# A two-layer encoder trunk on one core: another order of the work up to the first attention

## The reference

```
h    = rms_norm(x, attn_norm)                        # 256 x 1024
c_q  = rms_norm(h @ w_dq, g_cq)                      # 1024 -> 384
q    = (c_q @ w_uq).reshape(B, S, 16, 96)            # 384 -> 1536
kv_a = h @ w_dkv                                     # 1024 -> 288
c_kv = rms_norm(kv_a[..., :256], g_ckv)
k_pe = broadcast(kv_a[:, :, None, 256:])             # 32 rotary columns
kv   = (c_kv @ w_ukv).reshape(B, S, 16, 64 + 64)     # 256 -> 2048
k_nope, v = kv[..., :64], kv[..., 64:]
q = rms_norm(q, g_qn); k = rms_norm(concat(k_nope, k_pe), g_kn)
q, k = rope on the last 32 columns of each
o = block_causal_attention(q, k, v, 96 ** -0.5)
x = x + o @ w_o
```

## Time and profile before

| | |
|---|---|
| median of 3 runs | 1473.21 us (1472.29 to 1474.28) |
| the profiled execution | 1474.44 us, span 1472.6 us |
| busy in the span | TensorE 1420.9 us (96%), VectorE 1123.0, ScalarE 950.7, GpSimd 208.3 |
| HBM read | 430.95 MB |
| granted TensorE clock, mean of the span | 0.987 |
| share of the chain that ended last | TensorE 88%, VectorE 5%, DMA 2%, ScalarE 2% |

### The profile page before, as it was taken

How to read it: one execution, slowest core, us unless ns; L and a number is a source line. 1 busy time by engine, 2 the same in 40 slices (tenths; PEclk the granted TensorE clock), 3 DMA queues, 4 the chain that set the end, 5 groups by cost and what they waited for, 6 DMA issues and landing times.

```text
span 1472.6 us, 19787 instructions
## 1 busy us (share of the span) xinstructions
PE 1420.9 (96%) x7123; PEld 1202.1 (82%) x7123; DVE 1123.0 (76%) x986; ACT 950.7 (65%) x911; POOL 208.3 (14%) x145
## 2 busy tenths in 40 slices
PE   5899999999999799999999999999999999999997
PEld 5688899997877688888888888888888888888885
DVE  4576544446675688898899899888888889889985
ACT  4455443335553577777787687778777778678762
POOL 3120100000010323004003001200500400300322
PEclk9999999999999999999999999999999999999998
DMA  8144565554552499999999999999999999999994
GB/s 290 67 140 147 182 198 175 196 177 146 191 177 81 136 349 385 376 383 383 395 359 385 403 351 383 405 341 396 399 359 400 383 378 378 383 394 356 388 403 182
DMA packets 155442, 441.73 MB, mean 300 GB/s; under 512 B 11806, under 2 KB 41675, under 8 KB 155403
## 3 DMA queue, kind: packets, MB, share of 16 engines
q1 hardware_dynamic: 147296, 422.49, 77.0%
q0 software_dynamic: 4656, 15.03, 2.8%
q10 hardware_dynamic: 3450, 3.69, 0.8%
HBM read 430.95 MB, written 13.38 MB: 302 GB/s over the span
## 4 chain that ended last, share of the span: by engine, by line
PE 88%; DVE 5%; DMA 2%; ACT 2%; issue 2%; POOL 1%; POOLq 0%; ACTq 0%; SPq 0%; DVEq 0%
PE ps L1494 81%; PE ps L1489 4%; PE ps L1614 2%; DVE wl_a L1015 1%; PE ps L1634 1%; DMA y_rows<-ye,cur_s 1%; DVE wl_b L1015 1%; ACT wh_a L684 0%; ACT tn L693 0%; PE ps L1835 0%; DMA xr<-in_x 0%; DVE tn L1021 0%; DMA bias<-bias_wide 0%; DVE htl L1034 0%; DMA tn<-tn_rows,cur_g 0%
## 5 line engine op out<-in xcount | busy, mean ns | idle before, releaser
L1015 DVE TENSOR_TENSOR wl_a<-raw,wh_a 128x2048 fp32r<-128x2048 f32 (+1 forms) x230 | 515.9, 2269 | 122.8 <-ACT wh_a L684 122.7
L684 ACT ACTIVATE wh_a<-raw 128x2048 fp32r<-128x2048 f32 (+1 forms) x230 | 433.2, 1908 | 199.5 <-PE ps L1494 171.5
L1015 DVE TENSOR_TENSOR wl_b<-raw,wh_b 128x2048 fp32r<-128x2048 f32 x168 | 376.8, 2286 | 39.9 <-ACT wh_b L684 39.8
L684 ACT ACTIVATE wh_b<-raw 128x2048 fp32r<-128x2048 f32 x168 | 318.5, 1927 | 37.4 <-PE ps L1494 22.9
L1494 PE MATMUL ps<-wh_a,hth 128*128 128x512 f32 (+2 forms) x576 | 225.4, 391 | 8.5 <-DVE htl L1034 4.1
L1494 PE MATMUL ps<-wh_a,htl 128*128 128x512 f32 (+2 forms) x576 | 223.6, 388 | 0.0
L1494 PE MATMUL ps<-wl_a,hth 128*128 128x512 f32 (+2 forms) x576 | 223.5, 388 | 0.0
L1494 PE MATMUL ps<-wh_b,hth 128*128 128x512 f32 x448 | 175.0, 391 | 0.0
L1494 PE MATMUL ps<-wh_b,htl 128*128 128x512 f32 x448 | 174.5, 389 | 0.0
L1494 PE MATMUL ps<-wl_b,hth 128*128 128x512 f32 x448 | 174.3, 389 | 0.0
L1494 PEld LDWEIGHTS ps<-wh_a,hth 128*128 128x128 f32 x576 | 109.4, 190 | 30.2 <-issue 6.5
(11 more groups left out here) (259 smaller groups left out, 2190.7 us busy)
## 6 DMA issues: line engine op xcount, KB each, us to landing
raw<-in_moe_w SPq DMA_DIRECT2D x336, 1024.0 KB, 8.4
raw<-in_ffn_w SPq DMA_DIRECT2D x33, 1024.0 KB, 5.3
raw<-in_a_w_o SPq DMA_DIRECT2D x4, 1024.0 KB, 5.9
raw<-in_b_w_q SPq DMA_DIRECT2D x4, 1024.0 KB, 5.0
raw<-in_kv_w_k SPq DMA_DIRECT2D x4, 1024.0 KB, 5.0
raw<-in_kv_w_v SPq DMA_DIRECT2D x4, 1024.0 KB, 5.0
raw<-in_b_w_o SPq DMA_DIRECT2D x4, 1024.0 KB, 5.1
bias<-bias_wide ACTq DMA_DIRECT2D x8, 384.0 KB, 3.2
```

Source lines behind the costliest of these rows:

```text
L684: nc.scalar.activation(dst[:, 0:w], raw[:, n % RAW, 0:w], ACT.Copy).then_inc(hi_done, 1)
L1015: nc.vector.tensor_tensor(l[:, 0:w], raw[:, n % RAW, 0:w], h[:, 0:w].bitcast(fp32), ALU.subtract).then_inc(lo_done, 1)
```

## The change

The mathematics stays; lines numbered from here on are those of the changed kernel. Its parts:

- TensorE starts with six filler products as soon as the constants are there; the gains' transpose goes ahead of the rows' transposes, its copy ahead of the second block's scaling. ScalarE squares each block of x as soon as that block has landed.
- `turn_out("n0")` goes in two halves, with the halves of unit 1 between them.
- The transposes of the first three latent chunks go between the two w_dkv units, those of the last two between the first and the second w_uq unit; their splits are placed to match. GpSimd's root for the query latents goes ahead of its rotary tables.
- w_ukv is multiplied in another order: the key columns of both units first (each product reads 8 runs of 64 columns, one after every 128), then the value columns. A new semaphore `k_proj` counts the key tiles. The squares and sums follow each tile.
- The last four copies (values) go to the end: ScalarE's two ahead of `head_std`, VectorE's two behind `head_roots`.
- GpSimd rotates both blocks; its `kn` now also waits for the last unit of w_ukv.
- The filler ahead of attention 0 falls from 26 to 5 products. `hi(9)` goes behind `head_std`, `lo(9)` behind attention 0. The mask rows' loads wait for nothing (`qT` and `kT` lie 672 columns further on).

```diff
-BUSY = {"heads": 26, "n1": 8, "n2": 7, "n3": 12, "route": 3}
+BUSY = {"first": 6, "heads": 5, "n1": 8, "n2": 7, "n3": 12, "route": 3}
...
+        att.enter_context(nc.sbuf_tensor("late_gap", [P, 672], fp32))
         qT = sb("qT", [P, 2, 2 * SEQ], at=att)
...
         def latent_out(i):
+            src = ps[4 + i % 4][:, :]
             if i < 6:
-                return U_UQ + i // 2 + 1, q_all[:, i % 2, (i // 2) * 512:(i // 2 + 1) * 512]
-            k = (i - 6) // 2
-            return U_UKV + (i - 6) // 4 + 1, kv_all[:, i % 2, k * 512:(k + 1) * 512]
+                return unit_used, U_UQ + i // 2 + 1, q_all[:, i % 2, (i // 2) * 512:(i // 2 + 1) * 512], src
+            n, value = (i - 6) // 2 % 2, i >= 10
+            half = heads(kv_all[:, i % 2:i % 2 + 1, :], NOPE + VDIM, NOPE if value else 0, NOPE + VDIM if value else NOPE)
+            dst, src = half[:, 0, n * (HEADS // 2):(n + 1) * (HEADS // 2)], src.rearrange("p (h w) -> p h w", w=NOPE)
+            return (unit_used, U_UKV + n + 1, dst, src) if value else (k_proj, i - 5, dst, src)
...
-            sp.wait_ge(unit_used, U_UKV + 2)
             for tile_, at in ((qT, C_MA), (kT, C_MB - CHUNK)):
...
@@ GpSimd @@
+            pool.wait_ge(ss_lat, 2)
+            root(rstd[:, 0:T], ss[:, 0:T], Q_LORA).then_inc(rstd_lat, 1)
             pool.wait_ge(hg_here, 16 * 12)
...
-            pool.wait_ge(ss_lat, 2)
-            root(rstd[:, 0:T], ss[:, 0:T], Q_LORA).then_inc(rstd_lat, 1)
...
-            pool.wait_ge(sq_done[0], 2)
-            chain(rotate(nc.gpsimd, 1))
-            nc.gpsimd.tensor_tensor(q_rope(1), roptmp[:, 1, 0], roptmp[:, 1, 1], ALU.add).then_inc(rq_done, 1)
+            for t in range(T):
+                pool.wait_ge(sq_done[0], t + 1)
+                chain(rotate(nc.gpsimd, t))
+                nc.gpsimd.tensor_tensor(q_rope(t), roptmp[:, t, 0], roptmp[:, t, 1], ALU.add).then_inc(rq_done, 1)
...
             pool.wait_ge(rs_done[0], 1)
+            pool.wait_ge(unit_used, U_UKV + 2)
             attention(0)
@@ ScalarE @@
             hi(0)
-            hi(1)
             act.wait_ge(gcol_done, 1)
-            turn_out("n0", [(hth, G_ATT)])
+            turn_out("n0", [(hth, G_ATT)], (0, 1))
+            hi(1)
+            turn_out("n0", [(hth, G_ATT)], (2, 3))
...
+            out_even(0)
+            latent_hi(2, (3, 4))
+            hi(7)
+            out_even(2)
+            hi(8)
+            out_even(4)
+            for t in range(T):
+                act.wait_ge((pj_a, pj_v)[t][0], 3)
+                nc.scalar.activation(squares[:, t * HEADS * QK:(t + 1) * HEADS * QK], q_all[:, t, :], ACT.Square).then_inc(sq_done[0], 1)
+            out_even(6)
+            k_square(0, 0)
+            out_even(8)
+            k_square(0, 1)
+            k_square(1, 0)
+            k_square(1, 1)
+            out_even(10)
+            out_even(12)
...
             head_std(0)
+            hi(9)
@@ VectorE @@
-            normalise(0)
-            lo(0)
-
+            normalise(0, (0,))
             dve.wait_ge(gcol_tr, 1)
             nc.vector.tensor_copy(gcol[:], ps[7][:, 0:G_ALL]).then_inc(gcol_done, 1)
+            normalise(0, (1,))
+            lo(0)
+            dve.wait_ge(gcol_done, 1)
+            turn_out("n0", [(hth, htl, G_ATT)], (0, 1))
             lo(1)
-            dve.wait_ge(gcol_done, 1)
-            turn_out("n0", [(hth, htl, G_ATT)])
+            turn_out("n0", [(hth, htl, G_ATT)], (2, 3))
...
             head_roots(0, QK)
+            out_odd(11)
+            out_odd(13)
...
             for _ in attention(0):
                 pass
+            lo(U_WO0)
             turn_out("a0", [(hth, htl, None)])
@@ TensorE @@
-            turn("n0", [(tn_done, 1), (tn_done, 2)])
+            keep_busy(BUSY["first"], 6)
             pe.wait_ge(g_here, 16 * 5)
             tr(ps[7][:, 0:G_ALL], grow[:], G_ALL).then_inc(gcol_tr, 1)
-
+            turn("n0", [(tn_done, 1), (tn_done, 2)])
...
             for u, bank, w in ((U_DQ, 4, Q_LORA), (U_DKV, 6, KV_LORA + ROPE)):
                 for h in range(2):
+                    if u == U_DKV and h == 1:
+                        pe.wait_ge(lat_tn, 2)
+                        turn_latent((0, 1))
+                        turn_latent((2,))
                     ready(u + h)
...
+            pe.wait_ge(lat_l, 2)
             for n in range(3):
                 ready(U_UQ + n)
                 wh, wl = split_slot(U_UQ + n)
+                if n == 1:
+                    pe.wait_ge(lat_tn, 4)
+                    turn_latent((3, 4))
...
+            pe.wait_ge(lat_l, 3)
+            for part in (0, NOPE):
+                for n in range(2):
+                    ready(U_UKV + n)
+                    wh, wl = (a.rearrange("p (c h w) -> p c h w", c=KVC, w=NOPE + VDIM)[:, :, :, part:part + NOPE]
+                              for a in split_slot(U_UKV + n))
```

More of the change, by code:

```diff
@@ L271, in trunk_kernel @@
         unit_used = sem("unit_used")
-        x_here = sem("x_here")
+        x_here = [sem(f"x_here{t}") for t in range(T)]
+        k_proj = sem("k_proj")
         c_here = sem("c_here")
@@ L715, in _, with latent_hi @@
             act.dma_start(wr[:], rt_v).then_inc(wr_here, 16)
+            def latent_hi(b, chunks):
+                act.wait_ge(lat_tr, b + 1)
+                for c in chunks:
+                    last = nc.scalar.activation(ch[:, c, :], ps[c // 2][:, c % 2 * SEQ:(c % 2 + 1) * SEQ], ACT.Copy,
+                                                scale=gcol[:, G_CQ + c:G_CQ + c + 1])
+                last.then_inc(lat_h, 1)
             act.wait_ge(unit_used, U_DKV)
@@ L726, in _ @@
                                      accum_out=ss[:, T + t:T + t + 1]).then_inc(ss_lat, 1)
[L727 to L733 removed]
+            hi(6)
             act.wait_ge(lat_tn, 4)
@@ new lines, in out_even @@
+            def out_even(i):
+                made, n, dst, src = latent_out(i)
+                act.wait_ge(made, n)
+                nc.scalar.activation(dst, src, ACT.Copy).then_inc(pj_a[0], 1)
+            out_even(0)
[7 more added lines that the diff above has]
+                nc.scalar.activation(squares[:, t * HEADS * QK:(t + 1) * HEADS * QK], q_all[:, t, :], ACT.Square).then_inc(sq_done[0], 1)
@@ L1065, in _, with latent_lo, out_odd, q_sum @@
             ckv = tn[:, :, Q_LORA:Q_LORA + KV_LORA]
+            def latent_lo(b, chunks):
+                dve.wait_ge(lat_h, b + 1)
+                for c in chunks:
+                    last = nc.vector.scalar_tensor_tensor(cl[:, c, :], ps[c // 2][:, c % 2 * SEQ:(c % 2 + 1) * SEQ],
+                                                          gcol[:, G_CQ + c:G_CQ + c + 1], ch[:, c, :].bitcast(fp32),
+                                                          ALU.mult, ALU.subtract)
+                last.then_inc(lat_l, 1)
+            def out_odd(i):
+                made, n, dst, src = latent_out(i)
+                dve.wait_ge(made, n)
+                nc.vector.tensor_copy(dst, src).then_inc(pj_v[0], 1)
+            def q_sum(t):
+                dve.wait_ge(sq_done[0], t + 1)
+                nc.vector.reduce_sum(ssh[:, 0, t, :], squares[:, t * HEADS * QK:(t + 1) * HEADS * QK].rearrange("p (h w) -> p h w", w=QK),
+                                     AX).then_inc(sh_done[0], 1)
             dve.wait_ge(rstd_lat, 1)
@@ L1574, in _ @@
                         for c in range(KVC):
-                            at = c * 1024 + s * 512
                             last = mm3(ps[4 + i % 4][:, :], ch[:, QC + c, t * P:(t + 1) * P], cl[:, QC + c, t * P:(t + 1) * P],
-                                       wh[:, at:at + 512], wl[:, at:at + 512], c == 0, c == KVC - 1)
+                                       wh[:, c], wl[:, c], c == 0, c == KVC - 1)
+                        if part == 0:
+                            last.then_inc(k_proj, 1)
                         i += 1
-                last.then_inc(unit_used, 1)
+                    if part:
+                        last.then_inc(unit_used, 1)
             def attention(la):
```

113 lines of the change are left out of this document (36 added, 77 removed).

## The result

The changed kernel takes 1453.42 us (median of 4 runs, 1452.28 to 1453.69); the kernel before took 1473.55 us beside it (4 runs). The ratio is 0.9862, with a 95% interval of 0.9847 to 0.9876: faster by 1.4%. The profiled execution took 1453.61 us, with a span of 1451.7 where it was 1472.6.

A forecast was written before the change was run, and what follows sets the result against it. Expert layers keep TensorE busy, so the gain is what attention 0's earlier start brings: 21.2 us sooner, less 0.3 for unit 9, is -20.9; profiled 1474.44 becomes 1453.5, median 1452.3, range 1449 to 1457.5.

The forecast's parts named there:

- The start: Before the first weight product: constants at 5.8, six fillers until 11.1, then VectorE's queue; first product at 15.1 instead of 17.04.
- The 96 products: w_dq and w_dkv products: all at 2.4 GHz, 8.3 and 6.4 us, ending at 29.8.
- w_uq and w_ukv: The 102 products at 0.23 each plus transposes, 24.1 us, from 30.9 to 55.0.
- rival 2: Key and value products reading every other 64 columns of weights run slower, 10 us in all: 1462; chance 0.05.
- Last product to attention: ScalarE's value copy, table load and root, then VectorE's copies and scaled queries: attention at 61.1, not 82.27.
- on which the tail hung: Tail before attention: GpSimd rotating both blocks takes 4.4 us off VectorE's queue, said to have held the tail.
- GpSimd's rotations: Query rotation before attention: 4.7 us per block, both done at 55.1, needed at 60.3, so not on the path.
- Unit 9 behind attention: Low half moved behind attention 0 on VectorE: 0.2 us lost, with a hand-off 0.3.
- Attention's length: Attention 0 and what follows: unchanged, 1390.3 us from attention's start to the end.
- rival 1: Attention begins at a worse clock after TensorE idles about 4 us: +1 to +3, 1454.5; chance 0.14.
- hides nothing: Old filler ahead of attention, ending at 80.4: said to wait for none of the tail's chain and hide nothing.
- Rivals 3 to 5: GpSimd or halves late, 1455.5, 0.12; start filler fails to raise clock, 1454.9, 0.05; products all at 1.2 GHz, 1491, 0.02.

## Why the prediction was right, point by point

Predicted was 1452.3 us, within 1449.0 to 1457.5; measured 1453.42. Against the profiled execution the sum was -20.9 us, and the span fell by 20.9. The terms did not all hold: attention's start came 0.3 us sooner than worked out, unit 9 cost 0.3 less and the rest 0.2 less, against attention's 0.8. Each stage shortened by the mechanism that was forecast, but that the four errors cancel to nothing is luck.

- **The start**: 15.1 predicted, 15.18 measured, each link within 0.2: constants at 5.9, filler until 11.42, low half until 14.1. The gains were there in time (they had landed by 7.66 in the run without the filler). What the step did not see: the filler delays the first product by 1.65 us and is worth 0.45 net. w_dq ends at 23.76 where it ended at 27.92; with the filler giving 0.45 of these 4.2 us, the rest must lie in the new order of halves, blocks and transposes, which was not undone by itself.
- **The 96 products** at 2.4 GHz: 8.58 us for 48, 8.3 predicted. The step counted on stops of under 1 us ahead of them; the stop before the first was 1.45, and the level held. The start of w_uq: 30.9 predicted, about 31.2 measured (28.03 and 24 products of 0.133), with a wait of 0.22 at the transposes where 0.3 was taken. The run with the latents behind w_dkv shows the mechanism, gap and clock both.
- **w_uq and w_ukv**: 24.1 predicted, 23.7 measured, clock 1.00. The strided key and value products took 0.227 each (19.11 us for the chain's last 84, w_uq's among them), so rival 2 is out.
- **Last product to attention**: 6.1 predicted, 5.87 measured, with the links in the order that was forecast (copy 0.60, table 1.28, then root, copies, queries). This step named ScalarE's queue as last, "not the sums", and that is why GpSimd's rotation and the key order cost nothing when undone alone. The prediction credited the rotation's 4.4 us of VectorE's queue with the tail ("on which the tail hung"); that sentence failed. It holds for the kernel before, whose chain runs through that rotation, and is false once the other parts are in.
- **GpSimd's rotations**: 4.1 us per block, done at 54.4, where 55.1 was forecast from 4.7. The estimate from the Trainium skill (GPSIMD Engine Reference, Engine selection) was 3.5, from a VectorE operation that is no rotation. Against VectorE's own rotation, 2.9 us with about 0.9 of waiting for GpSimd in it, twice the rest would be an estimated 4.0, which agrees.
- **Unit 9 behind attention**: +0.3 predicted, 0.02 measured. The low half ends (105.06) just as ScalarE's high parts are ready.
- **Attention's length**: taken as unchanged, measured +0.8. This is rival 1, at less than its price: the first transposes do start low, and attention runs 9.1 us of its time low (60.76 to 69.9), where it ran 6.8 before (83.9 to 90.7). The rival's mechanism is right (13 fillers give 3.4 us back), and the sum should have carried part of it: the wait ahead of the stretch doubled from 1.8 to 3.7 us, which the rival itself had worked out. The sentence that the old filler "hides nothing" missed this: it hides no work, but a filler that reaches up to attention is worth 3.4 us in the changed kernel.
- **Rivals 3 to 5**: no stop of over 0.25 us lies among the products; the products run high from the first.

## What to carry to other kernels

Where several moves shorten one tail, undo them together as well as one at a time: here two cost nothing alone and three together cost 2.4 us, because ScalarE's queue ends about 2 us behind VectorE's and hides what VectorE is late by, up to that. Find in the profile of the changed kernel which queue ends last and by how much, and move that one next: here a table load that needed only to stand ahead of two copies (2.0 us at attention's start and 3.4 by the clock in its profile, 2.4 to 4.0 in the median). Filler products paid where they reached up to the next real work: eight more ahead of attention gave 3.4 us in the profile. Six ahead of a 3 us wait gave nothing that ten runs could tell.

## What the runs showed of the hardware

**VectorE and GpSimd hold each other up.** Two small operations of VectorE, 0.37 us in the run with VectorE's rotation and in the kernel before, took 1.28 in the changed kernel. Timeline of VectorE and of GpSimd there:

```profile
53.27 1.28 DVE L1133 TENSOR_SCALAR ssh<-ssh,ss 128x16 f32<-128x16 f32 x2
54.59 0.19 DVE L1139 TENSOR_SCALAR ssh<-ssh 128x64 f32<-128x64 f32 x1
```

```profile
53.10 1.29 POOL L571 TENSOR_TENSOR q_all<-roptmp 128x512 f32<-128x512 f32 x1
```

The first of the two alone took 1.15 us and ends at 54.42, 0.03 us behind GpSimd's operation; the second took 0.22. In the run with VectorE's rotation, in which GpSimd was done by 50.6, both are short. There the rotation itself meets GpSimd: its first operation takes 1.58 us, its last, of the same size, 0.69. GpSimd's operation and then these two:

```profile
49.30 1.29 POOL L570 TENSOR_TENSOR q_all<-roptmp 128x512 f32<-128x512 f32 x1
```

```profile
49.56 1.58 DVE L403 TENSOR_TENSOR roptmp<-q_all,ropt 128x512 f32<-128x512 f32 x1
...
51.84 0.69 DVE L1124 TENSOR_TENSOR q_all<-roptmp 128x512 f32<-128x512 f32 x1
```

It works the other way round too. Earlier in the changed kernel's execution, VectorE and GpSimd:

```profile
34.19 1.75 DVE L1027 TENSOR_TENSOR wl_a<-raw,wh_a 128x1536 fp32r<-128x1536 f32 x1
```

```profile
34.35 1.77 POOL L563 TENSOR_TENSOR roptmp<-kpe,ropt 128x64 f32<-128x64 f32 x1 [1.18 <-DVE tn L1111]
36.62 0.32 POOL L566 TENSOR_TENSOR kpr<-roptmp 128x64 f32<-128x64 f32 x1
```

An operation of GpSimd of the same size takes 0.32 us when VectorE is not in its low half, and 1.77 when it is. VectorE's sums (one input) and its copies out of PSUM are not held: 1.75 us for the sum beside a rotation as without one. And in the kernel before, where both engines rotated at once, GpSimd's block took 4.7 us instead of 4.1, VectorE's 4.4 instead of 2.9 (some 2.0 without the wait in it, an estimate from the rows above). The Trainium skill (SBUF — State Buffer, two separate sides) states it as an exclusive lock on a port pair that the two share, held for a whole instruction, which on VectorE's side takes an operation with two inputs from SBUF or in a fast mode; by that rule the first small operation and GpSimd's 1.77 us one had to wait for the other engine's whole instruction, and the trace agrees. Giving GpSimd work beside VectorE is therefore dearer than its own duration. The 0.9 us were hidden in the changed kernel, but not in the run with the root first, whose chain goes through them:

```profile
52.26 1.30 DVE ssh L1132 x2
```

**The clock's rise inside the filler is not the same in every execution.** The same twelve passes from 5.8 to 6.0 us on took 5.49, 5.49, 5.49 and 5.44 us in four profiles, 5.21 and 5.11 in two, 4.53, 4.36, 4.43 and 4.30 in four, and all that follows lies that much earlier. That is 1.2 us of the spread of some 3 us that runs of these kernels have.

**Where the clock falls is not settled.** In the changed kernel it had fallen when attention's first transpose came (eight in 1.96 us), in the run without the first filler it had not (1.09), with about the same wait of 3.7 us behind the same five fillers; there attention took 44.14 instead of 45.12 us. The edit lies 48 us ahead of it. Nor is the length of the wait enough: in the run with the root first a wait of 1.73 us kept the level through attention; in the kernel before one of 1.85 was followed by a fall 1.6 us into attention (low from 83.9 to 90.7); and in the kernel before with the filler at its start, with the same wait of 1.84 behind the same 26 fillers, the level stayed and attention took 41.76 us instead of 44.31. So attention's 3 us of clock are read from one execution of each kernel; that all eight runs with 13 fillers or with the root first lie below all nine of the changed kernel speaks for them. No run here says why.
